# Rotary embedding: the rotation by an exchange of partitions in place of a matrix product

## The chip, the core and the metric

The kernel runs on one core of a Trainium2 chip. The time is device time in microseconds (us) of one execution, from several runs; lower is better. Five engines work side by side, each with its own order of instructions: TensorE (matrix products; PE in the profile, PEld its weight loads), VectorE (DVE), ScalarE (ACT), GpSimd (POOL) and SyncE (SP), which issues DMAs. They wait for each other by semaphores.

## What is computed

One kernel computes a whole small model in float32: two layers of a diffusion block (feed-forward networks, a gated delta rule mixer, grouped attention) on 256 tokens and 256 context tokens, and then two hybrid layers with three attention branches (block attention, attention over positions picked by an index, attention over a memory). Two kinds of rotary embedding occur. In the first block, ten heads of width 128 (eight queries, two keys) are rotated over their whole width in neighbouring pairs:

```python
def apply_rope(x, cos, sin):
    x1, x2 = x[..., 0::2], x[..., 1::2]
    c, s = cos[:, None, :], sin[:, None, :]
    return jnp.stack([x1 * c - x2 * s, x1 * s + x2 * c], axis=-1).reshape(x.shape)
```

In the hybrid layers, heads of width 64 are rotated in their first 16 columns alone, 8 against 8:

```python
    x1 = x[..., :half]
    x2 = x[..., half:rot]
    return jnp.concatenate([x1 * cos - x2 * sin, x2 * cos + x1 * sin, x[..., rot:]], axis=-1)
```

There 21 tiles of two heads are rotated in each of the two layers: the index keys (1), index queries (4), and the queries and keys of two branches (16).

## The kernel before

Activations lie transposed, features on the 128 partitions and tokens along the row, 256 tokens for a rotated tile. Weights come as a stream: SyncE loads chunks of 512 KB into a ring of three (`ring`). Each half of a chunk (128 x 512) is split for precise products into a high part on ScalarE (`split_hi`, L2229) and a low part on VectorE or GpSimd (`split_lo`, L2475 and L2950), into four buffers `spl`. TensorE then makes three products for each weight tile (L1894, L1895, L1897 in `linear`; L1906 to L1908 in `by_token`); the eight tiles of one projection of 256 tokens use two halves. A split is three halves ahead of TensorE and waits until its buffer has been used.

The order of every engine comes from one generator, `order()`: it yields steps in one sequence, and each engine's program makes its instructions for the steps that it knows, in that sequence. `later` holds steps put off to the end of the next projection (`run_later`), `gens` holds attention and index work from which `pump` takes one piece between projections. So a step's place is the same for all engines, and an engine that waits in a step holds up all its later steps.

One rotation is the step `rope`. The tile to be rotated, `raw`, has been copied out of PSUM before (in the hybrid layers by `evacuate` on ScalarE, L2237, into one of two buffers `sqs`; in the first block by ScalarE's `head_gain` or VectorE's `head_unit`, and its scaling's root is ScalarE's L2257). At the end of the next projection TensorE multiplies it with a rotation matrix of 0, 1 and -1 (L2179), which swaps partners and sets the sign. VectorE multiplies the result with the sine table into a temporary `t` (one of three, `tmps`; L2864), GpSimd multiplies `raw` with the cosine table into the destination (L3007) after waiting for the matrix product, and VectorE adds `t` to it (L2867). The add frees `raw` and `t`.

In the memory attention of the hybrid layers one `pump` stands between two projections. In it come, for different heads, ScalarE's exponentials (L2415), VectorE's scaling of the probabilities (L2855, L2858), TensorE's product with the values (L2168), VectorE's product with the gate (`gate_out`, L2911), ScalarE's high part of that (L2233), TensorE's turning of the next probabilities (L2157), ScalarE's copy of the turned ones (L2422), and TensorE's next scores (L2146). Later, beside the second set of projections, VectorE searches the eight largest index scores again and again (L2896, L2900).

## Time and profile before

| | us |
|---|---|
| median of 3 runs | 2724.88 |
| lowest and highest | 2722.10, 2724.93 |
| span of the profiled execution, first to last instruction | 2720.2 |
| TensorE's matmuls busy in it | 2591.6 |
| VectorE, ScalarE, GpSimd busy | 1696.9, 1218.9, 666.8 |

The profiled execution is one more run. Its time is its span and what lies around it; set against the median of the runs, that is 4.7 us around the span. Busy times are shares of the span, sums over stages with different limits. The core's mean granted TensorE clock is 0.978 of 2.4 GHz.

### The profile page before, as it was taken

To read this page: it belongs to the slowest core of one execution; us is meant where nothing else is said; L and a number is where in the kernel's file an instruction comes from. 1 tells how busy PE (TensorE), PEld (TensorE's weight loads), DVE (VectorE), ACT (ScalarE), POOL (GpSimd) and SP (SyncE) were. 2 spreads that over 40 slices of the span, in tenths; PEclk is the share of its full clock that TensorE was granted. 3 is DMA by queue.
4 is the path that set the end of the run, shared out by engine and by line. 5 is a ranking of instruction groups with operands and counts; after the bars stand their busy time and mean duration, and the time that the engine had idled before them with its cause. 6 is when DMAs were issued, how large, how long until landed. Compare 5 with 4: busy or idle time off the path is not lost.

```text
span 2720.2 us, 43299 instructions
## 1 busy us (share of the span) xinstructions
PE 2591.6 (95%) x16792; PEld 2237.8 (82%) x16792; DVE 1696.9 (62%) x3011; ACT 1218.9 (45%) x2304; POOL 666.8 (25%) x604
## 2 busy tenths in 40 slices
PE   8999999997879999999999999999989999999998
PEld 5778887786777888787888887789988888989888
DVE  5776455898877666355654445665663567746666
ACT  4223323752153423323433224656545568555674
POOL 1011022003203111012111112121125543655335
PEclk9999999998889999999999999999999999999999
DMA  6554442220003453442443542335544443544434
GB/s 258 171 181 137 159 151 70 70 86 10 3 1 103 154 171 131 143 142 87 151 160 107 182 136 70 110 117 179 185 149 139 140 148 125 167 144 141 147 125 140
DMA packets 115868, 352.78 MB, mean 130 GB/s; under 512 B 12752, under 2 KB 14928, under 8 KB 115280
## 3 DMA queue, kind: packets, MB, share of 16 engines
q1 hardware_dynamic: 115664, 350.01, 38.2%
q8 instruction: 134, 2.20, 0.3%
q14 instruction: 70, 0.57, 0.1%
HBM read 348.91 MB, written 1.05 MB: 129 GB/s over the span
## 4 chain that ended last, share of the span: by engine, by line
PE 79%; DVE 7%; ACT 5%; DMA 3%; issue 2%; POOL 2%; SPq 1%; DVEq 0%; ACTq 0%; POOLq 0%
PE ps L1894 22%; PE ps L1897 21%; PE ps L1895 21%; DMA ring<-w_stream 2%; ACT spl L2229 1%; PE ps L1959 1%; PE ps L1936 1%; DVE big L2692 1%; DVE spl L2475 1%; PE ps L2146 1%; PE ps L1968 1%; PE ps L1906 1%; PE ps L1908 1%; PE ps L1907 1%; ACT big L2415 1%
## 5 line engine op out<-in xcount | busy, mean ns | idle before, releaser
L1894 PE MATMUL ps<-bigr,spl 128*128 128x256 f32 (+1 forms) x3880 | 1324.6, 341 | 35.9 <-DVE spl L2475 14.4
L1897 PE MATMUL ps<-bigr,spl 128*128 128x256 f32 (+1 forms) x3880 | 1303.4, 336 | 5.3 <-POOL bigr L2955 5.0
L1895 PE MATMUL ps<-bigr,spl 128*128 128x256 f32 (+1 forms) x3880 | 1301.0, 335 | 0.0
L2475 DVE TENSOR_TENSOR spl<-ring,spl 128x512 fp32r<-128x512 f32 x840 | 662.7, 795 | 665.2 <-ACT spl L2229 661.5
L2229 ACT ACTIVATE spl<-ring 128x512 fp32r<-128x512 f32 x1024 | 633.6, 627 | 811.5 <-PE ps L1897 619.6
L1894 PEld LDWEIGHTS ps<-bigr,spl 128*128 128x128 f32 x3880 | 740.2, 191 | 132.7 <-issue 28.8
L1897 PEld LDWEIGHTS ps<-bigr,spl 128*128 128x128 f32 x3880 | 739.9, 191 | 87.7 <-POOL bigr L2955 11.8
L1895 PEld LDWEIGHTS ps<-bigr,spl 128*128 128x128 f32 x3880 | 741.1, 191 | 73.9 <-issue 1.7
L2955 POOL TENSOR_TENSOR bigr<-work,bigr 128x512 fp32r<-128x512 f32 (+1 forms) x200 | 209.8, 1053 | 963.1 <-ACT bigr L2233 963.1
L2950 POOL TENSOR_TENSOR spl<-ring,spl 128x512 fp32r<-128x512 f32 x184 | 250.0, 1360 | 286.0 <-ACT spl L2229 285.3
L2233 ACT ACTIVATE bigr<-work 128x512 fp32r<-128x512 f32 (+2 forms) x240 | 123.4, 517 | 272.3 <-DVE work L2560 168.2
L2500 DVE SCALAR_TENSOR_TENSOR work<-big,small,work 128x512 f32<-128x512 f32 x175 | 125.9, 754 | 0.4
L2500 DVE SCALAR_TENSOR_TENSOR arow<-big,small,arow 128x512 f32<-128x512 f32 x161 | 115.1, 749 | 0.6
L2959 POOL TENSOR_TENSOR work<-work,X 128x512 f32<-128x512 f32 (+1 forms) x36 | 41.3, 1148 | 231.8 <-DVE X L2554 231.8
L2692 DVE SCALAR_TENSOR_TENSOR big<-big,prm 128x512 f32<-128x512 f32 x120 | 95.2, 834 | 0.0
L2560 DVE TENSOR_TENSOR work<-work,ps 128x512 f32<-128x512 f32 (+1 forms) x88 | 54.5, 619 | 54.4 <-PE ps L1897 41.4
L2253 ACT ACTIVATE work<-X 128x256 f32<-128x256 f32 (+1 forms) x80 | 39.3, 497 | 95.6 <-DVE X L2554 84.0
L2959 POOL TENSOR_TENSOR work<-work 128x512 f32<-128x512 f32 (+1 forms) x50 | 64.4, 1288 | 54.7 <-ACT work L2253 54.7
L1906 PE MATMUL ps<-spl,bigr 128*128 128x512 f32 (+1 forms) x128 | 51.7, 404 | 1.6 <-DVE spl L2475 1.0
L1968 PEld LDWEIGHTS ps<-cst,work 128*128 128x128 f32 x240 | 32.9, 202 | 24.5 <-POOL work L2959 7.0
L2554 DVE SCALAR_TENSOR_TENSOR X<-ps,small,X 128x256 f32<-128x256 f32 x80 | 35.5, 479 | 21.7 <-PE ps L1897 21.3
L2867 DVE TENSOR_TENSOR big<-big,work 128x256 f32<-128x256 f32 x52 | 30.8, 592 | 28.7 <-POOL big L3007 28.2
(309 smaller groups left out, 2432.3 us busy)
## 6 DMA issues: line engine op xcount, KB each, us to landing
ring<-w_stream SPq DMA_DIRECT2D x512, 512.0 KB, 3.4
big<-w_stream SPq DMA_DIRECT2D x256, 256.0 KB, 3.3
big<-w_stream SPq DMA_DIRECT2D x16, 512.0 KB, 11.6
X<-x_t SPq DMA_DIRECT2D x2, 1024.0 KB, 14.0
cst<-consts SPq DMA_DIRECT2D x1, 1537.5 KB, 7.1
X<-mem_t SPq DMA_DIRECT2D x1, 1024.0 KB, 5.7
out_t<-X SPq DMA_DIRECT2D x8, 128.0 KB, 2.2
prm<-params SPq DMA_DIRECT2D x1, 252.5 KB, 2.9
```

What stands on the lines that cost most here:

```text
L1894: pe.matmul(out, hi, x[0], start=k == 0, stop=False)
L1895: pe.matmul(out, lo, x[0], start=False, stop=False)
L1897: finish(pe.matmul(out, hi, x[1], start=False, stop=k == nk - 1), tile, key if k == nk - 1 else None)
L1906: pe.matmul(outs[i], src[0][:, a:b], hi, start=k == 0, stop=False)
L2229: act.activation(hi_half(h), raw_half(h), ACTF.Copy).then_inc(*sig("hi", h))
L2233: act.activation(hi, raw, ACTF.Copy).then_inc(*sig("dhi", u))
L2475: dve.tensor_tensor(lo_half(h), raw_half(h), hi_half(h), SUB).then_inc(*sig("lo", h, by="lo_dve"))
L2500: ins = dve.scalar_tensor_tensor(acc[s], slot, c, acc[s], MUL, ADD)
L2692: ins = dve.scalar_tensor_tensor(two(CF[m]), YP[m][:, :, j:j + 256], a, two(CF[m]), MUL, ADD)
L2950: pool.tensor_tensor(lo_half(h), raw_half(h), hi_half(h), SUB).then_inc(*sig("lo", h, by="lo_pool"))
L2955: pool.tensor_tensor(lo, raw, hi, SUB).then_inc(*sig("dlo", u, by="dlo_pool"))
L2959: ins = pool.tensor_copy(dst, src) if copy else pool.tensor_tensor(dst, dst, src, ADD)
```

## The change

TensorE's step and its rotation matrices go. ScalarE gets a step `rope` in the same place of the sequence: it waits until a temporary is free and `raw` is there, and issues DMAs from `raw` to `t` that exchange the partners' partitions. These are two DMAs for a tile of the first block (even rows to odd rows and the reverse, 64 rows of 1 KB each) and four for a tile of the hybrid layers (8 rows of 1 KB each). VectorE waits for the DMAs and multiplies `t` with the sine table in place; the signs are now in the table. The rows outside the rotated 16 keep what the temporary held, and their sine is 0. GpSimd's cosine product no longer waits for the rotation. Each temporary has a semaphore of its own for its DMAs, and no PSUM bank is taken.

```diff
-    out.append(("ropeS", np.repeat(np.sin(ang).T, 2, axis=0)))
...
+    out.append(("ropeS", np.repeat(np.sin(ang).T, 2, axis=0) * np.where(p % 2, 1, -1)[:, None]))
...
-            S[h + k] = S[h + 8 + k] = np.sin(ang[:, k])
-            R[h + k, h + 8 + k] = -1
-            R[h + 8 + k, h + k] = 1
+            S[h + k], S[h + 8 + k] = -np.sin(ang[:, k]), np.sin(ang[:, k])
...
-                    b, free, bi = banks.get()
                     t, tfree, ti = tmps.get()
-                    yield "rope", u, b, free, raw, need, names, t, tfree, out, ofree
-                    banks.give(bi, ("rope_s", u))
+                    yield "rope", u, raw, need, names, t, tfree, ti, out, ofree
...
-            def rope(u, b, free, raw, need, names, t, tfree, out, ofree):
-                w.all(free, done)
-                w.all(need, done)
-                pe.matmul(b[:, 0:L], P(names[0]), raw[:, 0:L], start=True, stop=True).then_inc(*sig("rot", u))
...
+            swapped = {"ropeC": [(slice(0, 128, 2), slice(1, 128, 2)), (slice(1, 128, 2), slice(0, 128, 2))],
+                       "prC": [(slice(h + a, h + a + 8), slice(h + 8 - a, h + 16 - a)) for h in (0, 64) for a in (0, 8)]}
+
+            def rope(u, raw, need, names, t, tfree, ti, out, ofree):
+                w.all(tfree, done)
+                w.all(need, done)
+                for to, of in swapped[names[0]]:
+                    act.dma_start(t[to, 0:L], raw[of, 0:L]).then_inc(*sig("rot", u, by=f"rot{ti}", n=16))
...
                 w.wait_ge(*done("rot", u))
-                w.all(tfree, done)
-                dve.tensor_tensor(t[:, 0:L], b[:, 0:L], P(names[2]), MUL).then_inc(*sig("rope_s", u))
+                dve.tensor_tensor(t[:, 0:L], t[:, 0:L], P(names[1]), MUL).then_inc(*sig("rope_s", u))
...
                 w.all(ofree, done)
-                w.wait_ge(*done("rot", u))
-                pool.tensor_tensor(out[:, 0:L], raw[:, 0:L], P(names[1]), MUL).then_inc(*sig("rope_c", u))
+                pool.tensor_tensor(out[:, 0:L], raw[:, 0:L], P(names[0]), MUL).then_inc(*sig("rope_c", u))
```

ScalarE's order in the memory attention of a hybrid layer, before: a pump with the split of the gated values and the copy of turned probabilities, two weight splits, the copy of the tile to be rotated, exponentials, and the next pump.

```order
L2233 ACTIVATE bigr<-work 128x256 [waits gate_out]
L2422 ACTIVATE big<-ps 128x512 [waits pt]
L2229 ACTIVATE spl<-ring 128x512 [waits used,arrived1]
L2229 ACTIVATE spl<-ring 128x512 [waits used]
L2237 ACTIVATE work<-ps 128x256 [waits rope,second_mm]
L2415 ACTIVATE big,small<-ps,small 128x256 [waits nmax]
L2415 ACTIVATE big,small<-ps,small 128x256
L2233 ACTIVATE bigr<-work 128x256 [waits gate_out]
L2422 ACTIVATE big<-ps 128x512 [waits av,pt]
```

The same place of ScalarE's order after the change (line numbers are the changed kernel's).

```order
L2218 ACTIVATE bigr<-work 128x256 [waits gate_out]
L2416 ACTIVATE big<-ps 128x512 [waits pt]
L2214 ACTIVATE spl<-ring 128x512 [waits used,arrived1]
L2214 ACTIVATE spl<-ring 128x512 [waits used]
L2400 DMA work<-work 8x256 [waits evac]
L2400 DMA work<-work 8x256 x3
L2222 ACTIVATE work<-ps 128x256 [waits rope,second_mm]
L2409 ACTIVATE big,small<-ps,small 128x256 [waits nmax]
L2409 ACTIVATE big,small<-ps,small 128x256
L2218 ACTIVATE bigr<-work 128x256 [waits gate_out]
L2416 ACTIVATE big<-ps 128x512 [waits av,pt]
```

Four DMAs now stand between the weight splits and the copy of the next tile.

VectorE's order in the same pump after the change: weight split, sine product (L2857), addition (L2860), scaling of the probabilities, gate product (L2904), and the largest scores.

```order
L2469 TENSOR_TENSOR spl<-ring,spl 128x512 [waits hi]
L2857 TENSOR_TENSOR work<-work,cst 128x256 [waits rot2]
L2860 TENSOR_TENSOR big<-big,work 128x256 [waits rope_c,rope_s]
L2849 RECIPROCAL small<-small 128x2 [waits exp]
L2852 TENSOR_SCALAR big<-big,small 128x256 [waits link]
L2852 TENSOR_SCALAR big<-big,small 128x256
L2904 TENSOR_TENSOR work<-ps,big 128x256 [waits rope,gated,av]
L2836 TENSOR_REDUCE small<-ps 128x2 [waits p,scores]
```

Nothing moved there: the sine product's operand and what it waits for are other, a DMA's semaphore (`rot2`) where a matrix product's stood.

## Rows read from the trace of the kernel before

**Rows 1.** The page's busy times: engine, us, share of the span, instructions.

```profile
PE 2591.6 (95%) x16792; PEld 2237.8 (82%) x16792; DVE 1696.9 (62%) x3011; ACT 1218.9 (45%) x2304; POOL 666.8 (25%) x604
```

**Rows 2.** Sine products (ns min/median/max, first to last), and rotations in the timeline: start, us.

```profile
L2864 DVE TENSOR_TENSOR work<-ps,cst x52: 397/416/426, 1678.9 to 2533.8; 128x256 f32<-128x256 f32 x52
...
2171.38 0.31 PEld L2179 LDWEIGHTS ps<-work,cst 128*128 128x128 f32 x2
2171.71 0.19 PEld L1894 LDWEIGHTS ps<-bigr,spl 128*128 128x128 f32 x1
...
2174.68 0.31 PEld L2179 LDWEIGHTS ps<-work,cst 128*128 128x128 f32 x2
```

**Rows 3.** SyncE: eight issues in a row; issue and landing of 256 KB, of 128 KB.

```profile
308.83 3.65 SPq L1855 DMA_DIRECT2D big<-w_stream  x8
...
L1850 SPq DMA_DIRECT2D big<-w_stream x216: 327/328/1342, 48.9 to 1601.3; - x108
...
DMA to landing us min/median/max: 2.5/3.0/7.6
...
L1864 SPq DMA_DIRECT2D out_t<-X x8: 348/446/454, 2713.5 to 2716.9; - x8
...
DMA to landing us min/median/max: 2.0/2.2/2.9
```

**Rows 4.** Stretches: us, busy of PE, PEld, DVE, ACT, POOL, granted clock, DMA share.

```profile
2063.00:2066.60 3.60, 3.60 (x19) 2.14 (x17) 1.38 (x4) 0.05 (x1) 2.65 (x3) 0.54 0.31 89
...
2092.00:2130.00 38.00, 37.49 (x264) 34.71 (x263) 18.29 (x45) 21.35 (x53) 19.72 (x20) 1.00 0.37 125
2158.00:2196.00 38.00, 38.00 (x261) 34.75 (x260) 23.80 (x67) 19.04 (x36) 22.82 (x21) 1.00 0.48 160
```

**Rows 5.** Timeline, one cycle of the memory attention, engine by engine.

```profile
2112.31 1.14 ACT L2229 ACTIVATE spl<-ring 128x512 fp32r<-128x512 f32 x2
...
2117.13 0.42 ACT L2233 ACTIVATE bigr<-work 128x256 fp32r<-128x256 f32 x1 [2.50 <-DVE work L2911]
2117.45 0.58 ACT L2422 ACTIVATE big<-ps 128x512 f32<-128x512 f32 x1
2117.93 1.14 ACT L2229 ACTIVATE spl<-ring 128x512 fp32r<-128x512 f32 x2
...
2114.77 0.73 POOL L3007 TENSOR_TENSOR big<-work,cst 128x256 f32<-128x256 f32 x1
...
2115.61 0.43 DVE L2867 TENSOR_TENSOR big<-big,work 128x256 f32<-128x256 f32 x1 [1.62 <-POOL big L3007]
2115.95 0.16 DVE L2855 RECIPROCAL small<-small 128x2 f32<-128x2 f32 x1
...
2116.68 0.42 DVE L2911 TENSOR_TENSOR work<-ps,big 128x256 f32<-128x256 f32 x1
...
2118.08 0.51 PEld L2168 LDWEIGHTS ps<-big 128*128 128x128 f32 x3 [0.79 <-ACT big L2422]
```

**Rows 6.** Timeline, ScalarE: splits at the four passes' start and end, both layers.

```profile
2106.88 0.63 ACT L2229 ACTIVATE spl<-ring 128x512 fp32r<-128x512 f32 x1 [0.75 <-PE ps L1897]
...
2127.26 1.14 ACT L2229 ACTIVATE spl<-ring 128x512 fp32r<-128x512 f32 x2
...
2448.51 0.63 ACT L2229 ACTIVATE spl<-ring 128x512 fp32r<-128x512 f32 x1 [0.87 <-PE ps L1897]
...
2467.58 1.14 ACT L2229 ACTIVATE spl<-ring 128x512 fp32r<-128x512 f32 x2
```

**Rows 7.** Timeline beside the top-8 search: ScalarE's split, VectorE's addition and split.

```profile
2173.56 0.63 ACT L2229 ACTIVATE spl<-ring 128x512 fp32r<-128x512 f32 x1 [0.96 <-PE ps L1897]
...
2173.51 0.43 DVE L2867 TENSOR_TENSOR big<-big,work 128x256 f32<-128x256 f32 x1 [0.37 <-POOL big L3007]
...
2175.16 0.95 DVE L2475 TENSOR_TENSOR spl<-ring,spl 128x512 fp32r<-128x512 f32 x1
```

**Rows 8.** Timeline, start of the first hybrid layer: the rotation that TensorE waits for.

```profile
2061.85 0.30 PEld L2179 LDWEIGHTS ps<-work,cst 128*128 128x128 f32 x2 [2.36 <-issue]
```

**Rows 9.** Timeline, first block: ScalarE's root and VectorE's addition of one head.

```profile
1702.73 0.26 ACT L2257 ACTIVATE small<-ps,cst 128x2 f32<-128x2 f32 x1 [1.09 <-PE ps L1968]
...
1704.22 0.43 DVE L2867 TENSOR_TENSOR big<-big,work 128x256 f32<-128x256 f32 x1 [0.53 <-POOL big L3007]
```

More of the change, by code:

```diff
@@ L115, in constant_list @@
     out.append(("ropeC", np.repeat(np.cos(ang).T, 2, axis=0)))
-    out.append(("ropeS", np.repeat(np.sin(ang).T, 2, axis=0)))
-    rot = np.zeros((128, 128))
-    for k in range(64):
-        rot[2 * k, 2 * k + 1] = -1
-        rot[2 * k + 1, 2 * k] = 1
-    out.append(("rotT", rot.T))
+    out.append(("ropeS", np.repeat(np.sin(ang).T, 2, axis=0) * np.where(p % 2, 1, -1)[:, None]))
     inv = np.float32(500000.0) ** (-np.arange(8, dtype=np.float32) / np.float32(8))
     ang = t.astype(np.float32)[:, None] * inv[None, :]
-    C, S, R = np.ones((128, L)), np.zeros((128, L)), np.zeros((128, 128))
+    C, S = np.ones((128, L)), np.zeros((128, L))
     for h in (0, 64):
@@ L128, in constant_list @@
             C[h + k] = C[h + 8 + k] = np.cos(ang[:, k])
-            S[h + k] = S[h + 8 + k] = np.sin(ang[:, k])
-            R[h + k, h + 8 + k] = -1
-            R[h + 8 + k, h + k] = 1
+            S[h + k], S[h + 8 + k] = -np.sin(ang[:, k]), np.sin(ang[:, k])
     out.append(("prC", C))
     out.append(("prS", S))
-    out.append(("prT", R.T))
     q = np.concatenate([p[:, None] + 128 * n >= np.arange(128 * n + 128)[None, :] for n in range(2)], 1)
@@ L1391, in headnorm @@
                         later.append(lambda: query_roots(m, n, sq, i, u))
-                        rope(raw, [("hu", u2)], ("rotT", "ropeC", "ropeS"), dst, f0, lambda t: raws.give(wi_, t), u2)
+                        rope(raw, [("hu", u2)], ("ropeC", "ropeS"), dst, f0, lambda t: raws.give(wi_, t), u2)
                         return
@@ L1413, in product @@
                             rest = [("hrest", u2)]
-                        rope(raw, [("hu", u2)], ("rotT", "ropeC", "ropeS"), dst, f0, lambda t: raws.give(wi_, t, *rest), u2)
+                        rope(raw, [("hu", u2)], ("ropeC", "ropeS"), dst, f0, lambda t: raws.give(wi_, t, *rest), u2)
                     later.append(stats_)
@@ L1556, in roped @@
                         banks.give(bi, ("evac",) + key)
-                        return rope(raw, [("evac",) + key], ("prT", "prC", "prS"), dst, need, lambda t: sqs.give(i, t))
+                        return rope(raw, [("evac",) + key], ("prC", "prS"), dst, need, lambda t: sqs.give(i, t))
                     def roped_proj(piece, m, dst, need):
@@ L2212, in tensor_program @@
                 gram, gate_rows, unit_turn, q_decay, level_p, level_u, u_values, w_keys, scan_v, scan_s, scan_own, head_turn,
-                scores, probs_turn, values, rope, index_weights, index_turn, index_heads)})
+                scores, probs_turn, values, index_weights, index_turn, index_heads)})
         def scalar_program(act, w):
@@ L2437, in scalar_program @@
                 gates_in, gates_exp, gates_ratio, short_conv, conv_silu, conv_glu, z_silu, tail_columns, turn_kv, decay, unit_turn, q_decay,
-                u_values, w_keys, tail_keys, scan_out, head_squares, conformer_silu, head_root, head_gain, head_unit, softmax, probs_turn, gated, index_heads)})
+                u_values, w_keys, tail_keys, scan_out, head_squares, conformer_silu, head_root, head_gain, head_unit, rope, softmax, probs_turn, gated, index_heads)})
         def vector_program(dve, w):
@@ L2859, in softmax, with rope @@
                     ins.then_inc(*sig("p", u))
-            def rope(u, b, free, raw, need, names, t, tfree, out, ofree):
+            def rope(u, raw, need, names, t, tfree, ti, out, ofree):
                 w.wait_ge(*done("rot", u))
-                w.all(tfree, done)
-                dve.tensor_tensor(t[:, 0:L], b[:, 0:L], P(names[2]), MUL).then_inc(*sig("rope_s", u))
+                dve.tensor_tensor(t[:, 0:L], t[:, 0:L], P(names[1]), MUL).then_inc(*sig("rope_s", u))
                 w.wait_ge(*done("rope_s", u))
@@ L3001, in head_rest, with rope @@
                 pool.tensor_copy(out, raw).then_inc(*sig("hrest", u))
-            def rope(u, b, free, raw, need, names, t, tfree, out, ofree):
+            def rope(u, raw, need, names, t, tfree, ti, out, ofree):
                 w.all(need, done)
                 w.all(ofree, done)
-                w.wait_ge(*done("rot", u))
-                pool.tensor_tensor(out[:, 0:L], raw[:, 0:L], P(names[1]), MUL).then_inc(*sig("rope_c", u))
+                pool.tensor_tensor(out[:, 0:L], raw[:, 0:L], P(names[0]), MUL).then_inc(*sig("rope_c", u))
             def index_start(l, IDX, need):
```

## The prediction, made before the changed kernel was run

> **What bounds the kernel now.** First the page's busy line: TensorE's matmuls are busy 95% of the span [rows 1]. On average, time taken from TensorE is time won, and time added elsewhere is free. The average is not enough here: the 52 rotations stand between 1679 and 2534 us [rows 2], so I then read TensorE's idle time, the stretches' windows and the timelines around single rotations. In the stretches with most of the rotations TensorE is busy 37.49 and 38.00 of 38 us, while ScalarE is busy 21.35 and 19.04 [rows 4]. There a second chain runs nearly as long as TensorE's. In one cycle of the memory attention (one projection, one head) [rows 5] ScalarE ends its two weight splits at 2113.45, GpSimd's cosine product follows from 2114.77 and ends the wait of VectorE's rope addition (2115.61). Behind it in VectorE's order stand the softmax scaling (2115.95) and the gate product (2116.68), on which ScalarE's split at 2117.13 waits. Behind that stand the copy of the turned probabilities (2117.45) and the next two weight splits (to 2119.07). TensorE waits 0.79 us for that copy. So this ring is at the limit already, and the change puts a DMA into it.
>
> **What is removed.** 52 rotation matmuls, one for each sine product. One takes TensorE from 2171.38 to 2171.71, 0.33 us [rows 2]; 52 x 0.33 = 17.2 us at most. GpSimd's cosine product waits for nothing of TensorE any more, and 52 bank turns go. The sine product on VectorE reads SBUF instead of PSUM, same size; I cost that at nothing, since VectorE waits at this place in either case.
>
> **What is added, one rotation's price.** ScalarE issues 4 DMAs of 8 rows (42 rotations) or 2 of 64 rows (10), 188 in all. The trace has no DMA on ScalarE and none between two places in SBUF, so both prices are bounded. Issue: SyncE issues 8 in a row in 3.65 us, 0.46 each, with a record of 0.33 for one [rows 3]. ScalarE waits in order, so I take 0.46; the lower end is 0.33, and nothing in this trace shows a cheaper one. The upper end is the longest ordinary median, 0.45, plus what ScalarE's own sequencer may add, to 0.6 as an estimate. Landing, from issue: at least 2.5 us for 256 KB, and 2.0 at least, 2.2 in the median for 128 KB [rows 3]. 8 to 64 KB lie below, so I take 1.95. No row reaches lower: I let the range go from 1.0 (half the shortest row, as nothing goes to or comes from HBM) to 3.0 (the median of a 256 KB load, if the packets queue behind the weights' at a DMA share of 0.37 [rows 4]). From the end of ScalarE's splits to data: 0.05 + 3 x 0.46 + 1.95 = 3.4 us for four DMAs, 2.4 for two.
>
> **Memory attention, four ring passes in each layer.** The order shows that ScalarE issues the DMAs behind its two splits, and that the gate product stands behind rope's two instructions on VectorE. A pass is then: 3.4 to the data, 0.45 for the sine product (0.42 [rows 2]) and its wait, 1.07 from the addition to the gate product, 2.39 from there to the end of the splits [rows 5], together 7.3 us. Two of four passes have no softmax scaling (2115.95 to 2116.68, 0.73 us): 6.6. Four passes: 27.8 us. Before, the pairs of splits end at 2107.51 and 2128.40 in the first layer, 20.9 us apart, and at 2449.14 and 2468.72 in the second, 19.6 [rows 6]. That is +6.9 and +8.2; in the second TensorE had 0.4 or so to spare, as an estimate, so I take +7.7. **+14.6 us.** TensorE, with about 4.6 us of work in a pass (19.6 / 4 less the rotation), waits; its saving there is inside the sum.
>
> **Projections beside the top-8 search, six rotations in each layer.** The pitch is 3.30 us (2171.38 to 2174.68 [rows 2], TensorE never idle), and would be 2.97. The ring goes over two projections: a split on ScalarE (0.63), the DMAs 3.4, sine product 0.45, from the addition to VectorE's weight split 1.65 (2173.51 to 2175.16), that split 0.95 [rows 7], and 0.1 to TensorE: 7.2 for two, 3.6 for one. +0.3 x 5 passes x 2 layers = **+3 us**. ScalarE's issues (1.84) beside 1.6 of other work (two splits and a copy) still fit into 3.6.
>
> **Start of each layer, five rotations.** TensorE waits 2.36 us at 2061.85 for a rotation whose source buffer was late [rows 8]. This wait goes, but ScalarE now issues 16 DMAs (7.4 us) before the copy that TensorE needs for turning the index weights. By adding up its queue I find TensorE's next projection starting about 1.4 us earlier, after an idle time of 4 us and more. After the 2.36 us wait the granted clock was 0.54 in a window of 3.6 us, so at the level of 1.2 GHz [rows 4]; a like drop now falls on denser work and takes back about 1.5. **0**, between -3 and +3.
>
> **Attention of the first block, ten rotations.** Where keys and queries are projected beside the scaled memory, VectorE's next scaling stands behind rope, and splits and matmuls behind that. The DMAs can go at 1702.99, land at 1705.4 (0.46 + 1.95), and the addition moves from 1704.22 to about 1705.85, +1.65 [rows 9]; a second place costs between 0 and that, I take 1.1. Against it 8 rotations x 0.33 = 2.6. **0.**
>
> **The other rotations,** six in each layer, are beside a TensorE that has nothing to wait for: 12 x 0.33 = **-4 us**. Sum: 14.6 + 3 + 0 + 0 - 4 = +13.6. The profiled execution has a span of 2720.2 us and the median is 2724.9; the 4.7 us around it don't change: 2738.
>
> One rule of the Trainium skill speaks against the change: "DMA: Bandwidth & Descriptors", Rules for kernel authors, says that many small transfers are to be coalesced, as under 64 KB one pays mostly overhead. No run so far shows such a transfer here; by that rule four DMAs for 32 KB are four overheads, of which the ring would have to wait for the last.
>
> **Rivals.** *Quick landing.* Nothing touches HBM, so the data may be there 1.0 us after issue. Each pass is 0.95 shorter: the ring passes cost +14.6 - 7.6 = +7, the top-8 projections become TensorE's again (12 x -0.33 = -4), the first block -2, the starts -2, the others -4: -5, so 2720. For it: the shortest landing falls with size; against it: from 256 to 128 KB it falls by 0.5 only. It decides where a landing is under about 1.3 us. The Trainium skill, "DMA: Bandwidth & Descriptors", Latency and other measured facts, gives about 0.6 us to a first byte of a DMA issued in this way; by it this rival would come true, and no row shows it. *All hidden.* If the gate product didn't have to wait, all 17 us come: 2708. The order speaks against it. *ScalarE becomes the bound.* At 0.6 us an issue, four take 2.4; with 1.6 of other work 4.0 in each top-8 projection, +0.4 x 12, and 0.45 more in each of 8 ring passes: +8; if besides TensorE's waits of near 3 us in each pass bring the 1.2 GHz level, as the 2.36 us did, its 4.6 us of work can outgrow the pass, by 1 us as an estimate, x 8. 2746 to 2756. *Slack takes it all.* The added waits fall into idle time of VectorE: it stood 1.62 us before that addition [rows 5], and the rest meets the saving: 2725.
>
> **How the numbers follow.** Forecast by rings 0.57 (2730 to 2746), ScalarE or clock 0.20, slack 0.09, quick landing 0.10, hidden 0.04. A difference under 0.2% (5.4 us) can't be told from none. Faster by more: 0.04 and half of quick landing, 0.09. Within: slack, the other half, and a little of the forecast's low end, 0.16. Slower 0.75. 8 in 10 lie in 2719 to 2756: this leaves out the hidden case and the far ends.
>
> **What would show it.** Memory attention: a sine product that starts 3.4 us after the splits' end, TensorE waiting 2 to 3 us for the probabilities' copy, pairs of splits 28 us apart over four passes. Top-8: pitch 3.6. On ScalarE, DMA rows at 0.46 pitch, 2 us to landing. Wrong if the landing is under 1.3 us, if ScalarE's issues take 0.1, or if the passes stay at 5 us.

## The result and the profile after

The changed kernel takes **2790.26 us** (median of 4 runs, 2784.8 to 2792.67), the kernel before 2723.49 us in the same comparison: ratio **1.0251**, 95% interval 1.0233 to 1.0269. The prediction had 2738 us and a range up to 2756: the sign was right, the size was 67 us in place of 14.

The page of the changed kernel: busy times, then the chain by engine, then the groups of VectorE's sine product (L2857) and ScalarE's copy out of PSUM (L2222), with the idle time in front of them. Lines of the code moved: split L2229 to L2214, VectorE's split L2475 to L2469, TensorE's L1894 to L1884, sine product L2864 to L2857, addition L2867 to L2860.

```profile
PE 2599.5 (93%) x16688; PEld 2245.3 (80%) x16688; DVE 1712.9 (61%) x3011; ACT 1218.2 (44%) x2304; POOL 668.3 (24%) x604
...
PE 73%; DVE 9%; ACT 6%; DMA 5%; issue 3%; ACTq 2%; POOL 1%; SPq 1%; DVEq 0%; POOLq 0%
...
L2857 DVE TENSOR_TENSOR work<-work,cst 128x256 f32<-128x256 f32 x52 | 31.4, 603 | 110.1 <-DMA work<-work 98.8
...
L2222 ACT ACTIVATE work<-ps 128x256 f32<-128x256 f32 (+1 forms) x44 | 16.5, 382 | 87.0 <-issue 40.8
```

The busy line [rows 1] hardly moved. VectorE stands 98.8 us in front of the sine product for data of the DMA (13.2 us for TensorE's rotation before). 40.8 us of idle time before ScalarE's copy are "issue": it waited for no other engine, and its own queue was issuing DMAs meanwhile.

What TensorE waits for in the stretch with the hybrid layers (waited for: us, times, longest), after, then before:

```profile
PE ps L1884 <- DVE spl L2469: 28.1, 15, 4.6
PE ps L2182 <- ACT work L2222: 14.1, 2, 7.2
PE ps L2158 <- ACT big L2416: 10.4, 5, 3.2
PE ps L1896 <- DVE spl L2469: 9.2, 5, 2.8
PE ps L2147 <- DVE big L2852: 6.5, 2, 4.1
```

```profile
PE ps L2179 <- ACT work L2237: 4.0, 2, 2.0
PE ps L1894 <- DVE spl L2475: 3.8, 5, 1.3
```

TensorE waits for VectorE's weight splits (37.3 us in 20 waits; 4.8 in 6 before), for ScalarE's copy of the index weights (L2182: 7 us once in each layer), and for the copy of the turned probabilities (L2158). The windows of the same work, before (503 us) and after (573 us), have PE, PEld, DVE, ACT, POOL busy, granted clock and DMA share:

```profile
2047.00:2550.00 503.00, 487.57 (x3609) 448.86 (x3609) 305.79 (x624) 296.28 (x611) 257.35 (x224) 0.99 0.44 147
```

```profile
2047.00:2620.00 573.00, 496.93 (x3520) 457.77 (x3521) 322.20 (x623) 294.54 (x612) 256.13 (x224) 0.94 0.40 131
...
2199.20:2202.80 3.60, 3.58 (x17) 3.59 (x18) 2.71 (x9) 0.88 (x2) 2.42 (x2) 0.54 0.45 150
```

TensorE's idle time grew from 15.4 to 76.1 us, by 60.6. Its busy time grew by 9.4, although 42 rotations (13.9 us) are gone. These 23 us fit longer matmuls at the lower granted clock (0.94 in place of 0.99); no run changes the clock alone. The second row shows one such place: 0.54 is near the level of 1.2 GHz, and just before it TensorE's matmuls had stood 2.83 and 2.27 us.

To find the stretch, I took the start of the same matmul of a projection in two traces. The table has the shift against the kernel before, gained in each stretch (us; times of before), for the changed kernel and three kernels of the experiments below. A wait at a border counts whole on one side of it: a jump of 4.9 us at 2103.98 is in the second row, one of 3.3 us at 2445.55 in the seventh. So a single row is sure to a few us only, while sums of neighbouring rows are surer.

```
stretch of before                     changed  issue only  no exchange  SyncE issues
2047-2074  start of layer 1             +3.2      +2.3        -6.1         -2.1
2074-2104  into memory attention        +5.2      +3.1        +0.4         +1.0
2104-2127  memory attention             +5.1      +0.9        +0.5         +0.5
2127-2160  values, gates                +9.6      +1.1        +0.5         +0.7
2160-2202  beside the top-8 search     +19.0      +1.7        +3.3         +3.5
2202-2416  rest, start of layer 2       +3.2      +2.7        -5.1         -3.8
2416-2446  into memory attention        +3.3      +3.1        -0.4         +3.1
2446-2468  memory attention             +7.5      +1.9        +0.2         +0.3
2468-2500  values, gates                +2.3      +1.1        +0.5         +0.5
2500-2542  beside the top-8 search     +11.4      -0.6        +1.8         +2.9
```

**One pass of the memory attention** in the changed kernel (start, us, engine, line), the answer to [rows 5]:

```profile
2125.86 0.42 ACT L2218 ACTIVATE bigr<-work 128x256 fp32r<-128x256 f32 x1 [3.48 <-DVE work L2904]
2126.18 0.58 ACT L2416 ACTIVATE big<-ps 128x512 f32<-128x512 f32 x1
2126.28 0.66 ACTq L2400 DMA_DIRECT2D work<-work  x1
...
2127.63 1.29 ACTq L2400 DMA_DIRECT2D work<-work  x2
...
2129.03 0.39 ACT L2222 ACTIVATE work<-ps 128x256 f32<-128x256 f32 x1 [1.23 <-issue]
...
2129.31 0.47 ACT L2409 ACTIVATE big<-ps,small 128x256 f32<-128x256 f32 x1
...
2130.09 0.43 DVE L2857 TENSOR_TENSOR work<-work,cst 128x256 f32<-128x256 f32 x1 [2.09 <-DMA work<-work]
...
2131.62 0.42 DVE L2904 TENSOR_TENSOR work<-ps,big 128x256 f32<-128x256 f32 x1
2132.07 0.42 ACT L2218 ACTIVATE bigr<-work 128x256 fp32r<-128x256 f32 x1 [1.74 <-DVE work L2904]
...
2132.59 0.63 ACTq L2400 DMA_DIRECT2D work<-work  x1
```

The four issues go from 2126.28 to 2128.92. They begin while ScalarE still copies (to 2126.76), so the queue runs ahead of the engine; but the copy L2222 and the exponents L2409 stand behind the last issue. The data are there 3.81 us after the first issue; addition, gate product and copy follow, and the pass is 6.31 us (2126.28 to 2132.59).

**Beside the top-8 search**, the answer to [rows 7]:

```profile
2189.70 1.09 DVE L2857 TENSOR_TENSOR work<-work,cst 128x256 f32<-128x256 f32 x1 [5.28 <-DMA work<-work]
2190.47 0.91 POOL L2999 TENSOR_TENSOR big<-work,cst 128x256 f32<-128x256 f32 x1
2190.82 0.83 DVE L2860 TENSOR_TENSOR big<-big,work 128x256 f32<-128x256 f32 x1
2191.58 1.58 DVE L2881 SCALAR_TENSOR_TENSOR big<-work,small,big 128x128 f32<-128x128 f32 x4
2191.69 2.61 ACTq L2400 DMA_DIRECT2D work<-work  x4
2193.08 0.68 DVE L2469 TENSOR_TENSOR spl<-ring,spl 128x512 fp32r<-128x512 f32 x1
...
2194.35 0.39 ACT L2222 ACTIVATE work<-ps 128x256 f32<-128x256 f32 x1 [5.21 <-issue]
...
2197.21 0.89 DVE L2857 TENSOR_TENSOR work<-work,cst 128x256 f32<-128x256 f32 x1 [3.44 <-DMA work<-work]
```

The sine product waits 5.28 us and takes 1.09 in place of 0.42. Behind it stand the addition, four products of the index scores (1.58 us) and then only the weight split at 2193.08, for which TensorE waits. The next four DMAs start at 2191.69, 0.04 us after the addition has ended (2190.82 + 0.83), 7.40 us after the first issue before them (2184.29).

### The profile page after: what moved, and what is told of

Same layout as the page of the kernel before. It is cut to its first block, busy times and chain, and to the rows that moved or that the text cites. A ratio compares the mean times of both kernels' runs of the same rounds, so it can differ in the third digit from the quotient of the medians.

```text
span 2790.8 us, 43200 instructions
## 1 busy us (share of the span) xinstructions
PE 2599.5 (93%) x16688; PEld 2245.3 (80%) x16688; DVE 1712.9 (61%) x3011; ACT 1218.2 (44%) x2304; POOL 668.3 (24%) x604
## 4 chain that ended last, share of the span: by engine, by line
PE 73%; DVE 9%; ACT 6%; DMA 5%; issue 3%; ACTq 2%; POOL 1%; SPq 1%; DVEq 0%; POOLq 0%
PE ps L1884 20%; PE ps L1887 20%; PE ps L1885 20%; DMA work<-work 2%; ACTq L2400 2%; DMA ring<-w_stream 2%; ACT spl L2214 2%; DVE spl L2469 1%; PE ps L1949 1%; PE ps L1926 1%; DVE big L2686 1%; PE ps L2136 1%; PE ps L1958 1%; ACT big L2409 1%; PE ps L1964 1%
## 5 line engine op out<-in xcount | busy, mean ns | idle before, releaser
L1884 PE MATMUL ps<-bigr,spl 128*128 128x256 f32 (+1 forms) x3880 | 1332.6, 343 | 60.6 <-DVE spl L2469 36.8
L2469 DVE TENSOR_TENSOR spl<-ring,spl 128x512 fp32r<-128x512 f32 x840 | 664.3, 797 | 657.2 <-ACT spl L2214 653.6
L2214 ACT ACTIVATE spl<-ring 128x512 fp32r<-128x512 f32 x1024 | 630.5, 627 | 802.9 <-PE ps L1887 600.4
L1884 PEld LDWEIGHTS ps<-bigr,spl 128*128 128x128 f32 x3880 | 749.6, 193 | 159.2 <-issue 35.7
L1887 PEld LDWEIGHTS ps<-bigr,spl 128*128 128x128 f32 x3880 | 748.7, 193 | 88.6 <-POOL bigr L2948 12.6
L1885 PEld LDWEIGHTS ps<-bigr,spl 128*128 128x128 f32 x3880 | 750.0, 193 | 74.0 <-issue 1.7
L2857 DVE TENSOR_TENSOR work<-work,cst 128x256 f32<-128x256 f32 x52 | 31.4, 603 | 110.1 <-DMA work<-work 98.8
L2222 ACT ACTIVATE work<-ps 128x256 f32<-128x256 f32 (+1 forms) x44 | 16.5, 382 | 87.0 <-issue 40.8
```

The lines of the kernel that those rows point to most:

```text
L1884: pe.matmul(out, hi, x[0], start=k == 0, stop=False)
L1885: pe.matmul(out, lo, x[0], start=False, stop=False)
L1887: finish(pe.matmul(out, hi, x[1], start=False, stop=k == nk - 1), tile, key if k == nk - 1 else None)
L2214: act.activation(hi_half(h), raw_half(h), ACTF.Copy).then_inc(*sig("hi", h))
L2469: dve.tensor_tensor(lo_half(h), raw_half(h), hi_half(h), SUB).then_inc(*sig("lo", h, by="lo_dve"))
```

## The experiments

All are timed against the kernel before on the same chip; its median was 2718.7 to 2723.5 us in the five comparisons, so differences between kernels of different comparisons are sure to some 3 us only. Each is a short edit of the changed kernel unless it says otherwise, and its edits hold for the hybrid layers alone. "Ratio" is to the kernel before.

```
kernel                                        us      ratio   95% interval
changed kernel                              2790.3   1.0251   1.0233-1.0269
no_exchange        no DMA, no wait          2713.9   0.9982   0.9973-0.9992
issue_only         DMAs, no wait            2734.2   1.0052   1.0036-1.0069
from_sync          SyncE issues             2724.3   1.0013   1.0000-1.0025
first_only         exchange in 1st block    2721.5   1.0002   0.9993-1.0012
early_act          ScalarE, right after copy 2768.6  1.0170   1.0149-1.0191
sync_behind_splits SyncE, behind the splits 2749.1   1.0111   1.0094-1.0128
half_dmas          two of four DMAs         2743.1   1.0085   1.0067-1.0103
few_weights        weight loads of 8 KB     2767.7   1.0175   1.0159-1.0190
own_target         other target buffer      2780.3   1.0225   1.0205-1.0245
early_sync         SyncE, right after copy  2782.1   1.0238   1.0220-1.0257
act_in_top8        ScalarE in top-8 only    2748.8   1.0099   1.0077-1.0122
before_few_weights before, loads of 8 KB    2720.4   1.0004   0.9994-1.0014
before_free_cos    before, one wait less    2717.8   0.9998   0.9988-1.0007
before_sbuf_sine   before, sine from SBUF   2727.9   1.0022   1.0009-1.0034
```

### Issue, wait, queue

**no_exchange.**

```diff
-                for to, of in swapped[names[0]]:
+                for to, of in swapped[names[0]] if names[0] == "ropeC" else ():
...
-                dve.tensor_tensor(t[:, 0:L], t[:, 0:L], P(names[1]), MUL)
+                dve.tensor_tensor(t[:, 0:L], (t if names[0] == "ropeC" else raw)[:, 0:L], P(names[1]), MUL)
```

> The changed kernel, but in the two hybrid layers (42 of the 52 rotations) nothing is exchanged: ScalarE issues no DMA there and VectorE's sine product reads the projection itself, so this part of the rotary embedding is left out of the computation. Theory A (VectorE stands in order in front of data that come too late) and theory B (the DMA issues hold up ScalarE's own weight splits) both expect the full saving of the rotation matmuls: 42 x 0.33 us = 14 us below the kernel before, 2708 to 2714 us. Theory C (the sine product from SBUF at 603 ns in place of 416, and the earlier cosine product, hold up VectorE and GpSimd) expects a good part of the loss to stay: above 2740.

Measured 2713.9. So the loss of 76 us to the changed kernel is all in the exchange itself, and theory C falls as its cause. But only 6.5 us were won by the medians (2 to 7 by the interval) where 14 were removed; that is taken up below.

**issue_only.** The DMAs go to `t[to, L:2 * L]`, VectorE reads `raw` as above, and the buffers are given back when the DMAs too are done.

> As the kernel without exchange in the hybrid layers, but ScalarE issues its four DMAs for each rotation at the same place, into a half of the buffer that nobody reads: the issue time (four in 2.64 us) and the traffic are there, the wait for the data is not (the exchange is left out of the computation). Theory A: little more than without exchange, 2710 to 2730 us. Theory B: most of the loss is here, 2765 us or more. The difference to the changed kernel is the price of waiting.

Measured 2734.2: the issues alone cost 20 us, the wait added to them 56 more. Theory A was nearer, B is not nothing. Much of the 20 us is one place, TensorE's wait for the index weights' copy at the start of each layer (the kernel without exchange shows no such wait):

```profile
PE ps L2183 <- ACT work L2223: 12.3, 2, 6.2
```

**from_sync.**

```diff
+            def rope(u, raw, need, names, t, tfree, ti, out, ofree):   # in sync_program
+                if names[0] == "prC":
+                    w.all(tfree, done)
+                    w.all(need, done)
+                    for to, of in swapped[names[0]]:
+                        sp.dma_start(t[to, 0:L], raw[of, 0:L]).then_inc(*sig("rot", u, by=f"rots{ti}", n=16))
```

> The changed kernel, but in the hybrid layers SyncE issues the four DMAs of a rotation, at the same place of the order, in place of ScalarE; VectorE waits for the data as before, the result is whole. ScalarE has its 2.64 us back; the data come from four serial issues on another queue. Theory A: the data come no earlier by more than a little (SyncE needn't wait for ScalarE's splits, so perhaps 1 us), 2765 to 2790 us. Theory B: ScalarE is free, so 2715 to 2740 us.

Measured 2724.3, as theory B said, although issue_only had just put B's part at 20 us. The trace of SyncE shows what both theories left out:

```profile
2103.69 2.66 SPq L1864 DMA_DIRECT2D work<-work  x4
2106.45 0.38 SPq L1815 DMA_DIRECT2D ring<-w_stream  x1
2110.04 2.68 SPq L1864 DMA_DIRECT2D work<-work  x4
```

Four issues take SyncE 2.7 us as well, but the first starts 0.07 us after ScalarE's copy (its end 2103.62), where ScalarE would first have gone through its splits. The kernel changed the queue and the place in time at once. early_act and sync_behind_splits below take them apart, though not fully.

**first_only.** TensorE turns in the hybrid layers as before.

> The exchange by DMA in the ten rotations of the first block only; in the hybrid layers TensorE turns as before the change, and GpSimd waits for it as before. Both theories and my term for the first block (0): within 3 us of the kernel before, 2721 to 2727 us. If it is above 2730, part of the loss is made in the first block, against what the compared traces show (no shift of TensorE's matmuls over 1.5 us there).

Measured 2721.5, ratio 1.0002: the first block costs nothing.

**early_act.**

```diff
+                        yield "swap", u, raw, [("evac",) + key], i
...
+            def swap(u, raw, need, i):   # in scalar_program
+                w.all(need, done)
+                for to, of in swapped["prC"]:
+                    act.dma_start(raw[to, L:2 * L], raw[of, 0:L]).then_inc(*sig("rot", u, by=f"rots{i}", n=16))
```

> The changed kernel, but in the hybrid layers ScalarE issues the four DMAs right behind the copy of the projection out of PSUM, ahead of the work that follows and of the next weight splits (into the other half of the copy's own buffer, from where VectorE reads them at the same place of its order as before). Result whole. The runs so far: without exchange 2713.9, issue alone 2734.2, issue and wait 2790.3, issue by SyncE right behind that copy, with the wait, 2724.3 us. Theory P (place: the data are late because the issues stand behind ScalarE's splits, 2.64 + 1.8 to 4.5 us before VectorE can go on): the data now come a projection earlier, the waits go, what stays is the issue time: 2728 to 2742 us. Theory Q (queue: ScalarE's 2.64 us of issuing delay its splits wherever they stand, and with the splits the whole ring): 2775 to 2800 us.

**sync_behind_splits.** As from_sync, with one line ahead of the DMAs: `w.wait_ge(*done("hi", last[0]))`, the last but one split of ScalarE in the order.

> The kernel in which SyncE issues the exchange in the hybrid layers, but SyncE now waits for the last but one of ScalarE's weight splits ahead of the rotation, so that the DMAs go where ScalarE's went in the changed kernel, with ScalarE free. Theory P (place): the wait for late data costs VectorE as much as in the changed kernel, less the 20 us that the issuing alone cost: 2760 to 2785 us. Theory Q (queue): ScalarE is free, so 2720 to 2735 us. In between, by sum of the two: each gives part.

Measured 2768.6 and 2749.1, both between the two theories. What ended VectorE's idle time before the sine product (us, times), first early_act, then sync_behind_splits; in the changed kernel it is 98.8 in 34:

```profile
L2865 DVE TENSOR_TENSOR work<-work,cst x52: 398/935/1525, 1683.5 to 2581.1; 128x256 f32<-128x256 f32 x52
...
  DMA work<-work: 7.8, 8
```

```profile
L2870 DVE TENSOR_TENSOR work<-work,cst x52: 397/426/1511, 1675.4 to 2560.4; 128x256 f32<-128x256 f32 x52
...
  DMA work<-work: 61.8, 31
```

With ScalarE issuing early the wait for data is nearly gone (7.8 us), and 48 us of loss are left. Here ScalarE's own work is held up: its exponentials now stand behind the issues, for example

```profile
2116.87 2.62 ACTq L2407 DMA_DIRECT2D work<-work  x4
2119.53 0.47 ACT L2416 ACTIVATE big<-ps,small 128x256 f32<-128x256 f32 x1 [2.70 <-issue]
```

With SyncE issuing late, ScalarE is free, the wait stays at 61.8 us, and 29 us of loss are left. In one table (us):

```
                      behind the splits   right after the copy   difference
ScalarE issues             2790.3               2768.6              21.7
SyncE issues               2749.1               2724.3              24.8
difference                   41.2                 44.3
```

Queue and place nearly add up here: about 43 us for the queue, 23 for the place. But the four kernels are not one edit apart. The early ScalarE kernel has another target buffer (own_target below), and from_sync issues behind the next weight loads where early_act issues at once. The kernel that differs from early_act by the queue alone is early_sync below, and it took 2782.1, not 2724. So the last column is no general price of the queue.

"Queue" also hides two things. Besides freeing ScalarE, SyncE's order keeps the weight loads away from the exchange. From the last of four issues to the sine product that waits for it, the changed kernel has a median of 2.25 us, with 19 of 34 over 2.0; sync_behind_splits has 1.79, with 1 of 31 over 2.0. One rotation of each (the last of four issues starts 2.0 us after the first):

```profile
2103.44 2.62 ACTq L2400 DMA_DIRECT2D work<-work  x4
2105.49 0.33 SPq L1812 DMA_DIRECT2D ring<-w_stream  x1
2108.80 0.43 DVE L2857 TENSOR_TENSOR work<-work,cst 128x256 f32<-128x256 f32 x1 [5.39 <-DMA work<-work]
```

```profile
2102.63 2.66 SPq L1870 DMA_DIRECT2D work<-work  x4
2105.39 0.38 SPq L1815 DMA_DIRECT2D ring<-w_stream  x1
2106.46 0.43 DVE L2870 TENSOR_TENSOR work<-work,cst 128x256 f32<-128x256 f32 x1 [2.52 <-DMA work<-work]
```

On ScalarE's queue a weight load of SyncE starts 0.07 us after the last issue, and the data take 3.38 us. On SyncE's own queue the next load starts 0.7 us after it, and the data take 1.8 us.

**half_dmas.** `for h in (0, 64)` becomes `for h in (0,)`.

> The changed kernel with two of the four DMAs in the hybrid layers (heads in rows 0 to 63 only; the exchange for the other half of the heads is left out of the computation). Issue 1.32 us in place of 2.64, and the last issue lands 1.32 us earlier. If the loss of 76 us against the kernel without exchange goes with the number of issues: 2745 to 2760 us. If the landing time behind weight loads rules and not the number: over 2770 us. Under 2735: the ring needs only part of the time and the loss sets in above a threshold.

Measured 2743.1: half the issues take 47 of the 76 us away. The loss goes with the number, somewhat more than in proportion. The Trainium skill, "DMA: Bandwidth & Descriptors", Rules for kernel authors, asks to coalesce small transfers; this run fits it, with 47 us for two DMAs fewer in each of 42 rotations, but it moves half the bytes too, and no run has the same bytes in fewer DMAs.

### Landing, target, place in SyncE's queue

**few_weights** and its control **before_few_weights**: from the first hybrid layer on, `sp.dma_start(place(c)[:, 0:n], W[c][:, 0:n])` with n = 16.

> The changed kernel with the weight loads from the first hybrid layer on cut from 512 KB to 8 KB each (their number and place stay; old values stay in the buffers, so these layers compute with wrong weights). Landings from the last issue are then 1.80 us everywhere if the long ones (2.2 to 4.5 us) were packets behind weights. Over the 42 rotations this is some 0.9 us each, 38 us; those in the rings count, so 2755 to 2775 us. If landing behind weights doesn't matter: 2785 us or more. A control of the kernel before with the same cut follows.

> Control: the kernel before the change with the weight loads from the first hybrid layer on cut to 8 KB, as in the changed kernel that took 2767.7 us with this cut, 22.6 us less than without. If the cut helps by shorter landings of the exchange alone: the kernel before stays at 2718 to 2723 us. If the kernel is waiting for weights or their traffic slows the engines: it falls by as much, below 2710 us.

Measured 2767.7 and 2720.4 (ratio 1.0004): the changed kernel wins 22.6 us by it, the kernel before nothing, so it is the landing. Where VectorE waited, the time from the last of four issues to the sine product falls from the median of 2.25 us to 1.81, with 3 of 33 over 2.0 (the longest 3.25). The sum of the waits there falls from 98.8 to

```profile
  DMA work<-work: 72.6, 33
```

The Trainium skill, "DMA: Bandwidth & Descriptors", Queues, rings and completion order, says that the queues' rings take turns on the same DMA engines, packet by packet; the two runs agree.

**own_target.**

```diff
-                    act.dma_start(t[to, 0:L], raw[of, 0:L])
+                    act.dma_start(t[to, 0:L] if names[0] == "ropeC" else raw[to, L:2 * L], raw[of, 0:L])
```

> The changed kernel, with ScalarE's DMAs at the same place, but in the hybrid layers they write into the unused half of the projection's own copy, which is free by construction, in place of a shared work buffer for which ScalarE may have to wait (one issue in the search beside the top-8 starts 0.03 us behind the addition that frees its buffer). VectorE waits for the work buffer instead, as before the change. If that wait on the target buffer is a main part of the loss: 2765 to 2780 us. If it is met now and then only: 2783 to 2792 us.

Measured 2780.3, between the two. The intervals of the ratios (1.0205 to 1.0245, and 1.0233 to 1.0269) overlap: the wait for the target is worth some 7 to 10 us at most and isn't a main part. By this, the place alone is worth some 12 us on ScalarE (2780.3 to 2768.6), not 22.

**early_sync.** The `swap` of early_act, issued by SyncE.

> Both changes of place and queue, and the target of its own: SyncE issues the exchange right behind the copy out of PSUM, into the other half of the same buffer; VectorE reads it where it did before. Result whole. The four kernels so far add up: ScalarE behind its splits 2790, ScalarE early 2769, SyncE behind the splits 2749, SyncE early 2724 us; without exchange 2714. With no wait for the target the DMAs can go earlier still: 2716 to 2723 us. Equal to 2724 if the target's buffer was always free.

Measured 2782.1: a clear miss of 60 us. ScalarE's splits over the hybrid layers, early_sync and then from_sync:

```profile
L2224 ACT ACTIVATE spl<-ring 128x512 fp32r<-128x512 f32 x278 | 169.7, 627 | 204.9 <-DMA ring<-w_stream 121.1 <-PE ps L1897 69.6 <-PE ps L1908 13.6
```

```profile
L2224 ACT ACTIVATE spl<-ring 128x512 fp32r<-128x512 f32 x280 | 171.8, 628 | 125.2 <-PE ps L1897 73.8 <-DMA ring<-w_stream 27.2 <-PE ps L1908 23.7
```

They wait 121.1 us for weights in place of 27.2. In from_sync the exchange stands in SyncE's order behind the next projection's weight loads, here ahead of them: while SyncE waits for the copy, the loads wait with it. I had named the place and not what is queued behind it. Against early_act, which differs by the queue alone, SyncE is here some 14 us slower.

**act_in_top8.** from_sync, with ScalarE issuing behind its splits for the eight rotations of the second set of queries and keys.

> SyncE issues the exchange as in the kernel that took 2724.3 us, except for the eight rotations in each layer of the second set of queries and keys (beside the top-8 search): those ScalarE issues behind its splits, as in the changed kernel. Result whole. In the changed kernel TensorE's matmuls move back by 19.0 and 12.1 us over these stretches, in the kernel with SyncE by 3.5 and 3.6: if this loss is made there and not carried in from the memory attention, 24 us come on top, 2742 to 2754 us. If it only appears there because the rings were disturbed before, under 2735 us.

Measured 2748.8, 24.5 us above from_sync. Its matmuls move back by 14.4 and 13.5 us in the two stretches beside the top-8 search (from_sync 3.5 and 2.9), so the loss is made there and not carried in. Here too ScalarE's held-up work and the longer landings on its queue come together.

### Parts of the change alone

**before_free_cos.** The kernel before, without `w.wait_ge(*done("rot", u))` in GpSimd's rope.

> The kernel before the change with one wait less: GpSimd's cosine product doesn't wait for TensorE's rotation (it needs nothing of it). Result whole. This is the one part of the change that costs nobody anything: the ring of the memory attention waits 1.62 us for the cosine product in each pass, but TensorE is idle there 0.5 us in 38 only: 0 to 3 us less than before, 2717 to 2721 us. If the early cosine product collides with VectorE's work: up to 3 us more.

Measured ratio 0.9998: nothing that can be told.

**before_sbuf_sine.**

```diff
-                dve.tensor_tensor(t[:, 0:L], b[:, 0:L], P(names[2]), MUL)
+                dve.tensor_tensor(t[:, 0:L], (raw if names[0] == "prT" else b)[:, 0:L], P(names[2]), MUL)
```

> The kernel before the change, TensorE's rotation and all waits kept, but in the hybrid layers VectorE's sine product reads the projection's copy in SBUF in place of the rotation in PSUM (so the rotation has no effect on the result). Same size, same time of start. In the kernels with the operand in SBUF this product takes up to 1.53 us (over 0.6 us in 13 of 42 in the changed kernel, in 27 of 42 without exchange), with it in PSUM 0.42 us always. If it is the operand's place, together with GpSimd's products at the same time: mean from 0.42 to 0.8 or 0.9 us, and 2 to 8 us more, 2722 to 2728 us. If it is only the different time of the product: it stays at 0.42 us, and 2718 to 2721 us.

Measured 2727.9, +7.7 us by the medians (ratio 1.0022, so 2 to 9 us by the interval; four of the ten runs lie at 2719 to 2722, six at 2727 to 2731). The 42 sine products, kernel before and then this one (ns, min/median/max):

```profile
L2864 DVE TENSOR_TENSOR work<-ps,cst x42: 409/416/426, 2059.5 to 2533.8; 128x256 f32<-128x256 f32 x42
```

```profile
L2864 DVE TENSOR_TENSOR work<-work,cst x42: 412/951/1531, 2061.2 to 2539.9; 128x256 f32<-128x256 f32 x42
```

Same size, nearly the same waits (12.0 us in 13 in place of 12.6 in 14), another place of one operand: the median goes from 0.42 to 0.95 us, the longest from 0.43 to 1.53. All 24 products over 0.6 us overlap an instruction of GpSimd, as do 12 of the 18 short ones; with the operand in PSUM 36 of 42 overlap one and none takes over 0.43. In the changed kernel, 2189.70 and 2190.47 above show such a pair: VectorE's product beside GpSimd's. The size is enough to explain why taking the rotations out whole gave 6.5 us and not 14. The Trainium skill, "GPSIMD Engine Reference", Specifications, says that GpSimd's SBUF interfaces are shared with VectorE and contend with its instructions that have two SBUF inputs; the rows agree.

No version with the exchange beats the kernel before: with DMAs in the first block alone it is at 1.0002, and the best one with DMAs in the hybrid layers too, from_sync, at 1.0013.

## Why the prediction was right or wrong

**What bounds the kernel, the ring, the sign: right.** Adding waits of VectorE and ScalarE around TensorE's work made the kernel slower although TensorE lost work.

**"I cost that at nothing" (the sine product from SBUF): wrong.** I looked only at whether VectorE waits there, not at who else reads SBUF at that time. before_sbuf_sine puts it at 7.7 us (2 to 9).

**Issue, 0.46 us each, upper end 0.6: wrong.** Measured for the 8-row and the 64-row DMAs:

```profile
L2400 ACTq DMA_DIRECT2D work<-work x168: 631/632/1834, 2059.4 to 2603.5; - x168
L2400 ACTq DMA_DIRECT2D work<-big x20: 472/609/622, 1677.6 to 1751.2; - x20
```

The pitch is 0.66 us, four take 2.6, above even the upper end of 0.6. SyncE needs as long for the same four, so it isn't ScalarE's sequencer; I had taken the price from DMAs of another form [rows 3].

**Landing, 1.95 us, range to 3.0: right when the queues are quiet, too short otherwise.** 1.80 us at the least; mean 2.53 where VectorE waited, up to 3.81. The bound "if the packets queue behind the weights'" stood in the prediction as an end of the range, when 19 of 34 took over 2.0 us; few_weights prices it at 22.6 us. Quick landing falls with it: it took the time to a first byte for the time to the data, and the shortest wait for data was 1.80 us.

**Memory attention, +14.6 us: right in size, in part by luck.** Measured +5.1 and +7.5, together 12.6. The pass of 7.3 or 6.6 us was 7.92, 6.31, 5.32, 5.21 and 7.11, 6.62, 6.96, 6.14 from first issue to first issue, in sum 24.8 and 26.8 in place of 27.8 each. Two errors cancel in it: the DMAs go ahead of the splits' end, since ScalarE's queue runs ahead (in the pass shown the sine product starts 2.3 us after it, not 3.4), and each takes longer.

**Beside the top-8 search, +3 us: the step that failed most.** Measured +19.0 and +11.4, and act_in_top8 shows that 24 us of it are made there. The ring was priced at 7.2 us for two projections, 3.6 for one. That left out four things, all in the rows above: the issues at 0.66; the longer landing; the sine product and addition at 1.09 and 0.83 us; and the index products and the wait for the target buffer, by which one rotation can follow the other. So a pass could be 7.40 us for one projection. How the 30.4 us divide among the four was not measured, except that own_target puts the wait for the buffer at 10 us at most in the whole kernel.

**Start of each layer, 0: wrong, +6.4 together** (without exchange -11.2). I had counted ScalarE's 16 issues at 7.4 us; they take 10.6, and the copy of the index weights for which TensorE waits stands behind them. That the issues do it is shown: this wait of TensorE is 14.1 us in the changed kernel, 12.3 with the issues alone, 2.1 in sync_behind_splits:

```profile
2068.14 4.61 ACTq L2400 DMA_DIRECT2D work<-work  x7
2072.79 0.37 ACT L2222 ACTIVATE work<-ps 8x256 f32<-8x256 f32 x1 [4.47 <-issue]
```

**The other rotations, -4 us: wrong, +20.4** (5.2 + 9.6 + 3.3 + 2.3). "TensorE has nothing to wait for" was true of the trace before. Its cover was the lead of VectorE's weight splits over the matmuls, and a wait of 5 us in front of a split can use this lead up. The lead itself was not measured; what the trace shows are the 37.3 us of waits for L2469, here and beside the top-8 search.

**First block, 0: right as a sum** (first_only, 1.0002); its two terms of 2.7 and 2.6 us were not measured apart.

**The rivals.** "ScalarE becomes the bound, the clock drops" was the mechanism nearest to what came: moving the issues to another queue takes 41 us away (of which landings may be up to 22.6), and the longer matmuls are about 23 us (the two overlap). I gave it 8 to 18 us over the forecast (its own terms add up to 16), since I let it act in the 20 passes of two stretches and not at each rotation. "Slack takes it all" is what the kernel with SyncE does, with another queue. The sum of the stretches is 12.6 + 30.4 + 6.4 + 20.4 = 69.8 us, and the profiled spans differ by 70.6.

**Two readings of mine** were of weight loads: the 0.79 and 2.36 us that TensorE "waits" at [rows 5] and [rows 8] are idle time of its loads. Its matmuls waited 0.39 and 1.99 us there. For the sum this is 0.4 us in each layer at most.

**What stays open.** The 76 us have no single experiment that divides them. Three runs give parts that nearly add up: issuing alone 20 (issue_only), late data with ScalarE free and quick landings 35 (2749.1 against 2713.9), the longer landings on ScalarE's queue 22.6 (few_weights), together 78. But each was measured in another kernel, and the parts depend on the place: in early_act ScalarE's issues leave a loss of 55 us against no_exchange with hardly any wait for data. How the 22 us of the early kernel's difference divide between target buffer and place is settled only to within the 7 to 10 us of own_target.

## What to carry to other kernels

A DMA in place of a small matmul is priced by its whole way: issues times their number on a queue that works in order, landing behind whatever else flows, and everything that stands behind the waiting instruction; here 0.33 us of TensorE became 3.8 to 5.8 us of a chain, once 7.1. Before putting a wait into an engine's order, ask how far ahead its other products are used, not whether the consumer waits today. If such a DMA must be, issue it from a queue whose owner computes nothing, as soon as its source is written, but behind the loads that others live on: all three together took 2790 us to 2724 here, and without the last (and with another target buffer) it was 2782. Putting the exchange into the loads' own queue also kept the loads from starting beside it.

## What the runs showed of the hardware

- An SBUF to SBUF DMA of 8 rows by 1 KB takes its queue 0.66 us on ScalarE and 0.68 on SyncE, against 0.33 to 0.46 for the loads and stores of [rows 3]; with 64 rows the records are 0.47 and 0.61.
- From the last issue to the waiting product: 1.80 us at the least, up to 3.81 with ScalarE issuing. In the changed kernel 12 of the 13 over 2.9 us had a weight load issued by SyncE between 0.9 us before and 0.3 us after the last issue, and none of the 15 under 2.0 had; with the exchange on SyncE's own queue (sync_behind_splits) 30 of 31 took 1.78 to 1.88 us.
- ScalarE's queue issues DMAs while the engine still works on earlier instructions (2126.28 against 2126.76), but instructions behind the issues wait for them (1.23, 4.47 and 5.21 us marked "issue"; 2.70 in early_act).
- VectorE's 128x256 product of two SBUF operands takes up to 1.53 us beside GpSimd's work (before_sbuf_sine), with one operand in PSUM never over 0.43 in the kernel before.
